# Three feed-forwards of a two-block network on Trainium2: the extra modulation block's parts, one in each of four steps

## The reference, cut to what matters

```python
def swiglu(h, w_in, w_out):
    gu = h @ w_in
    g, u = jnp.split(gu, 2, axis=-1)
    return (jax.nn.silu(g) * u) @ w_out

mods = jnp.split(c_silu @ ada_w[layer] + ada_b[layer], N_MOD, axis=-1)
sh, sc, g = mods[0], mods[1], mods[2]
h = modulate(rms_norm(x, norm_g[layer, 0]), sh, sc)
x = x + MACARON_WEIGHT * (1.0 + g)[:, None, :] * swiglu(h, ffn_w_in[layer, 0], ffn_w_out[layer, 0])
```

## Time and profile before

| | us |
|---|---|
| median of 3 runs | 1292.15 |
| profiled execution | 1290.39 |
| span of its instructions | 1288.6 |
| PE busy | 1236.0 |
| DVE busy | 1082.9 |
| ACT busy | 670.6 |

### The profile page before, as it was taken

The page is one execution under the profiler, slowest core; times in us unless marked ns, Lnnn a source line. Parts: engine busy times, 40 slices in busy tenths (PEclk is TensorE's granted clock), DMA queues, the critical chain, the costliest instruction groups (busy, mean ns, idle before and its releaser), DMA issues.

```text
span 1288.6 us, 26536 instructions
## 1 busy us (share of the span) xinstructions
PE 1236.0 (96%) x10414; PEld 1202.9 (93%) x10414; DVE 1082.9 (84%) x1670; ACT 670.6 (52%) x1129; POOL 167.4 (13%) x195
## 2 busy tenths in 40 slices
PE   2999999899999999999999999999999999999997
PEld 1999999799999988999999999999999989999996
DVE  6998988898888877989988879999987588896575
ACT  2543344554444555654447764444466665355453
POOL 4599910000000000000001000000000004220000
PEclk8999999999999999999999999999999999999999
DMA  9999897489888459988863389887656699546562
GB/s 360 384 331 317 314 312 279 165 303 329 310 308 304 145 180 354 318 320 304 308 235 120 116 262 338 305 306 266 216 180 197 114 189 174 170 143 211 180 192 83
DMA packets 111357, 320.26 MB, mean 249 GB/s; under 512 B 24272, under 2 KB 35984, under 8 KB 110992
## 3 DMA queue, kind: packets, MB, share of 16 engines
q1 hardware_dynamic: 111248, 318.76, 74.3%
HBM read 313.70 MB, written 5.02 MB: 247 GB/s over the span
## 4 chain that ended last, share of the span: by engine, by line
PE 80%; DVE 12%; ACT 3%; DMA 2%; issue 2%; SPq 1%; DVEq 0%; ACTq 0%
PE quad L409 16%; PE quad L410 16%; PE quad L411 16%; PE acc L409 8%; PE acc L411 8%; PE acc L410 8%; DVE w_lo L401 3%; DVE arena L1619 2%; ACT w_hi L397 1%; PE quad L625 1%; PE quad L599 1%; PE quad L627 1%; DMA x<-in_x_t 1%; DMA land<-in_stream 1%; DVE x L1741 1%
## 5 line engine op out<-in xcount | busy, mean ns | idle before, releaser
L397 ACT CAST w_hi<-land 128x1024 fp32r<-128x1024 f32 x391 | 409.4, 1049 | 357.0 <-PE quad L411 234.8
L401 DVE TENSOR_TENSOR w_lo<-land,w_hi 128x1024 fp32r<-128x1024 f32 x391 | 485.1, 1246 | 117.1 <-ACT w_hi L397 114.8
L409 PE MATMUL quad<-xs_hi,w_hi 128*128 128x256 f32 (+1 forms) x1384 | 392.1, 283 | 0.8 <-DVE arena L2148 0.5
L411 PE MATMUL quad<-xs_hi,w_lo 128*128 128x256 f32 (+1 forms) x1384 | 390.5, 282 | 0.0
L410 PE MATMUL quad<-xs_lo,w_hi 128*128 128x256 f32 (+1 forms) x1384 | 389.8, 282 | 0.0
L409 PEld LDWEIGHTS quad<-xs_hi,w_hi 128*128 128x128 f32 x1384 | 261.1, 189 | 3.1 <-issue 0.9
L410 PEld LDWEIGHTS quad<-xs_lo,w_hi 128*128 128x128 f32 x1384 | 261.9, 189 | 0.1
L411 PEld LDWEIGHTS quad<-xs_hi,w_lo 128*128 128x128 f32 x1384 | 261.2, 189 | 0.0
L1619 DVE SCALAR_TENSOR_TENSOR arena<-arena 128x1024 f32<-128x1024 f32 x184 | 227.0, 1240 | 12.0 <-ACT arena L1329 8.6
L409 PE MATMUL acc<-h_hi,w_hi 128*128 128x256 f32 x704 | 196.9, 280 | 1.8 <-DVE h_lo L1669 1.4
L411 PE MATMUL acc<-h_hi,w_lo 128*128 128x256 f32 x704 | 196.7, 279 | 0.0
(11 more groups left out here) (365 smaller groups left out, 1682.1 us busy)
## 6 DMA issues: line engine op xcount, KB each, us to landing
land<-in_stream SPq DMA_DIRECT2D x391, 512.0 KB, 4.5
arena<-in_gstream SPq DMA_DIRECT2D x184, 512.0 KB, 6.1
w_dram<-arena SPq DMA_DIRECT2D x3, 512.0 KB, 6.3
arena<-w_dram SPq DMA_DIRECT2D x6, 256.0 KB, 9.8
arena<-in_c_rows SPq DMA_DIRECT2D x2, 512.0 KB, 5.4
x<-in_x_t SPq DMA_DIRECT2D x1, 1024.0 KB, 10.3
arena<-in_ssm_bn SPq DMA_DIRECT2D x1, 1024.0 KB, 5.5
u_dram<-arena SPq DMA_DIRECT2D x1, 1024.0 KB, 5.3
```

Of the source, the lines that this page charges most:

```text
L397: nc.scalar.copy(w_hi[:, u % RING], land[:, u % LAND]).then_inc(hi_done, 1)
L401: nc.vector.tensor_tensor(w_lo[:, u % RING], land[:, u % LAND], w_hi[:, u % RING].bitcast(F32), ALU.subtract).then_inc(lo_done, 1)
L409: nc.tensor.matmul(outs, lh, rh, start=first, stop=False, **kw)
L411: last = nc.tensor.matmul(outs, ll, rh, start=False, stop=end, **kw)
```

## The change

On DVE the four parts E0 to E3 no longer stand at the first and the third unit of the first two steps, but one at the first unit of each of the four steps. On SP the count that the loads of C0 to C3 wait for is that of the new order: 1, 4, 7 and 10 parts of these blocks instead of 1, 3, 5 and 7. C0 and C1 are loaded in the third step (at its first and second unit), C2 and C3 in the fourth.

```diff
@@ block.sync: SP
                             for s in range(3):
                                 if vector and s < 2:
                                     if beside is not None and m >= 2:
-                                        sp.wait_ge(g_done, 4 * beside + 2 * (2 * (m % 2) + s) + 1)
+                                        sp.wait_ge(g_done, 4 * beside + 3 * (2 * (m % 2) + s) + 1)
                                     g_load(b + m // 2, 2 * (m % 2) + s, i)
@@ block.vector: DVE, ffn
-                                if G_FIRST[f] and part == 0 and m < 2 and s != 1:
-                                    g_part(b - 1, 2 * m + s // 2, vector)
+                                if G_FIRST[f] and part == 0 and s == 0:
+                                    g_part(b - 1, m, vector)
```

## The result

The changed kernel takes 1309.81 us (median of 4 runs, 1307.17 to 1312.43) beside 1291.86 us of the kernel before; the ratio is 1.0149, 95% interval 1.013 to 1.0168. It is slower by 18 us, as forecast. Its profiled execution took 1310.86 us with a span (first instruction to last) of 1309.1 us, 20.5 us over the span of before.

The account below looks back on a forecast made before the run. The prediction took TensorE, 96% busy, as the bound, with DVE close behind. Lateness of 15.7 us plus 2.8 for the clock made 18.5 on 1290.39, so 1308.9, or 1311 for the runs' median; range 1301 to 1320.

Parts of the forecast that it names:

- The direction and the place: Slower, 95%; fourth-step PE waits at output units in the second and third feed-forwards, before an up unit in the first.
- second short wait: First feed-forward: after the up-unit wait, PE waits again before the output unit, which starts at 88.3 against 84.08.
- The chain's length: Second feed-forward, third part's end to the hidden tile's low part: 17.6 us, with two load landings of 4.8 each.
- The lateness: PE's delay at the fourth step: 4.2, 5.7 and 5.8 us in the three feed-forwards, 15.7 together.
- waits of rows 4: PE's 0.4 to 0.5 us waits for a hidden tile's low half at the second step, forecast to vanish.
- The clock: Half clock behind PE's new waits: 1.2 us each in the second and third feed-forwards, 0.4 in the first; 2.8 together.
- Rival 3: Second and third feed-forwards: PE waits only for the up unit's split, losing 2.4 and 2.5 us; 1302 us; 6%.
- rival 2: Landings behind a modulation load take 5.9 us, as on the loaded queue: 1317.3 us; 14%.
- rival 1: PE's waits come as forecast but the clock stays up, 2.8 us less: 1308 us; 20%.
- Rival 4: Not slower: the waits are hidden, only the second-step waits go, a gain of 1.4 us: 1290.8 us; 5%.
- SP's waits: SP's waits for modulation parts rise from 3.9 and 17.8 us to some 65 together, about 6 and 9 per feed-forward.
- With nothing in between: Fourth step's loads: two load latencies come one after the other, with the four landing slots already empty.

Follow-up runs that it names:

- counts-alone: The kernel before with SP's new counts 1, 4, 7 and 10 but DVE's old order: 1304.21 us, ratio 1.0117.
- own-queue: The changed kernel with the second and third feed-forwards' last two quarter loads issued from GpSimd's queue instead of SP's: 1294.69 us, ratio 1.0042.
- 3, 4, 3 and 2 parts: Against the kernel before: the four parts at the first step, twice in the second, and the third's first unit; counts 1, 4, 6, 8: 1289.29, again 1288.01 us.
- only E3 late: Against the changed kernel: second and third parts both in the second step, last part still in the fourth, counts 1, 4, 6, 10: 1309.21 us, ratio 1.0156.
- E ahead of the split: The changed kernel with each step's part ahead of the step's first split on DVE instead of behind it: 1303.06 us, ratio 1.0114.

## Why the prediction was right, point by point

**The direction and the place.** Right. The waits were forecast at the output units in the second and third feed-forwards, released by `h_lo`, near 297 to 299 and 538 to 541, and before the up unit in the first near 85; they end at 302.20, 551.19 and 84.30. The later two are the forecast places plus what the earlier feed-forwards had lost by then. The second short wait forecast in the first didn't come: its output unit starts at 88.76 without one. The up unit ahead of it had taken 4.5 us instead of 2.8, with a granted clock of 0.61 over it. The counts-alone and own-queue kernels show that it is SP's queue.

**The chain's length.** 17.6 us from E2's end to the low part forecast, 17.4 in the trace (from 284.64 to 302.06). Its one estimated term, the landing at 4.8, was 5.05 both times, between the ends 3.6 and 5.9. The rest was 8.0 forecast, 7.3 measured.

**The lateness.** 4.2, 5.7 and 5.8 us forecast without the clock; in the trace 5.7 at the third's output unit, and for the second 8.1 less the clock's 2.3, 5.8. The first came 4.7 late with a clock part of 0.4 forecast, 4.6 in all. The waits of rows 4 went, as forecast.

**The clock.** The mechanism was right, the term mis-sized: 1.2 us for each long wait was forecast, 2.3 and 2.4 measured. Two things made it too small. I had taken one stretch of 3.40 us, while here the clock was already at half when PE came back and stayed so for the whole of the output unit, 5.0 us. And I had read that row too low: its 19 matmuls include two that began before the stretch, so 17 began in it, 12 too few and not ten, which is 1.4 us. The same place without the fall (last section) takes 1.5 us less. The Trainium skill, in "TensorE: Matmul & The Clock Gate", Terms, prices the time at half clock at one half. Taken over the 5.0 us in which PE worked at half clock that is 2.5, and the trace agrees with it (2.3 and 2.4). Taken over all of the half clock, with the 1.9 us in which PE still waited, it would be 3.4, and the trace doesn't agree.

**The sum.** 15.7+2.8 = 18.5 forecast on the profiled execution; by the rows above 4.7+8.1+8.1 = 20.9, and 20.5 by the spans. The excess over the forecast is the clock's. The runs' medians are 18.0 apart. The two profiled executions stood low (before) and high (after) among their runs, by 1 to 1.5 us each, so the medians' 18.0 is less than what the traces hold, and part of the closeness of 1311 to 1309.81 is luck.

**The rivals.** Rival 3 (PE waits for the split, not for the low part) fell with the low part put ahead, rival 2 (landings of 5.9 us) with the landings at 5.05, rival 1 (the clock stays up) with the clock's row. Rival 4 (no loss) needed landings of 2.0 us.

**SP's waits** for parts were to rise to some 65 us; they are 75.7. The prediction left one out: E1 moves too, so C1's load waits for it. In the second feed-forward SP is done with the load before it at 272.4 us and issues C1 at 276.47, and this stands beside the 6.7 and 8.4 us for C2 and C3 that were forecast as 6 and 9. This third wait delays nothing that PE needs: the kernel with 3, 4, 3 and 2 parts has it too.

One step of the argument was weaker than it read: that the two landings come one after the other is true of the chain, but DVE stood only 1.05 us for the first, and the kernel with only E3 late loses as much. Most of the loss is one landing with E3 too late ahead of it. "With nothing in between" was wrong: DVE's work of the third step is.

## What to carry to other kernels

Evening out an engine's work by moving a consumer later also moves the moment at which its buffer comes free; if one engine issues the loads in program order and waits in between, look first at what stands behind the refill, and only then at the refill itself. Put each part that frees a buffer early enough that its count is reached before the next load could leave anyway. Here a unit's load may leave when the unit four places ahead of it is split, so the part should stand no later than at that unit, as in the kernel with 3, 4, 3 and 2 parts. An estimate of a wait of an otherwise full TensorE should allow for time at half clock behind it, at the price of the work that falls into it.

## What was not expected of the hardware

The granted clock doesn't follow from a wait's length alone. Behind 1.94 us of waiting it fell (0.56 over 3.90 us, above). Behind 2.30 in the counts-alone kernel it did not, nor behind 3.49 in the kernel with E ahead of the split:

```profile
299.80:303.70 3.90, 3.88 (x33) 1.00 1.03 418
```

```profile
296.30:300.20 3.90, 3.90 (x33) 1.00 1.03 420
```

At the third feed-forward's head the same wait of 2.56 us comes in every trace. The clock falls with it in those of before and after, but not in the own-queue kernel's. Of the two traces of one and the same kernel, with 3, 4, 3 and 2 parts, it stays up in the first and falls in the second:

```profile
441.50:445.40 3.90, 3.90 (x32) 1.00 0.68 220
```

```profile
441.50:445.40 3.90, 3.90 (x20) 0.57 0.72 215
```

From that wait to PE's next one there are 22.6 us in the two traces in which it stays up, and 24.1 in the eleven others. What decides between them stays open. It is one source of 1.5 us between executions of one kernel.
